# Where the down lows, the first block's weight sums, the token loads and the normalising of a conv-FFN stand on their engines

## The reference, cut to what matters

```python
def conv_ffn(h, conv_hist, w_up, w_dw, b_dw, w_down):
    up = h @ w_up                                   # 1024 -> 2 * 2816
    ext = jnp.concatenate([conv_hist.astype(up.dtype), up], axis=1)
    c = ext[:, 0:T] * w_dw[0] + ext[:, 1:T + 1] * w_dw[1] + ext[:, 2:T + 2] * w_dw[2] + b_dw
    a, b = jnp.split(c, 2, axis=-1)
    return (jax.nn.silu(a) * b) @ w_down, ...       # 2816 -> 1024
...
    x2 = layer_norm(ALPHA * x1 + ffn + ple, ln2_g, ln2_b)
```

## Time and profile before

| what | us |
|---|---|
| median of 3 runs (lowest, highest) | 3042.74 (3041.82, 3044.16) |
| the profiled execution | 3045.18 |
| its span, first to last instruction | 3043.4 |
| busy in the span: PE, DVE, ACT, POOL | 2853.6, 2110.9, 1451.0, 1066.3 |

### The profile page before, as it was taken

One profiled execution on the slowest core, in us unless ns is written; L12 is line 12 of the kernel. 1 busy time (PEld: TensorE's weight loads), 2 busy tenths in 40 slices (PEclk: granted clock), 3 DMA queues, 4 the chain that ended last, 5 costly groups with the idle time before them and its releaser, 6 DMA issues. The chain is left out here.

```text
span 3043.4 us, 47351 instructions
## 1 busy us (share of the span) xinstructions
PE 2853.6 (94%) x14597; PEld 2481.4 (82%) x14597; DVE 2110.9 (69%) x3081; ACT 1451.0 (48%) x2947; POOL 1066.3 (35%) x816
## 2 busy tenths in 40 slices
PE   8998999999999899999899999988999997999996
PEld 6877787777777688887798988878999996888885
DVE  5635776777776444445687877797777778788776
ACT  4342555877787222222453444443544544455553
POOL 5341544766676433334433333210111111111113
PEclk9997998999999999999999999989999998999998
DMA  4226452222113333334633324344323334533331
GB/s 136 87 69 145 139 167 56 43 62 47 43 43 129 129 104 103 103 103 147 206 108 103 118 91 133 116 142 161 100 93 117 100 94 137 183 121 119 107 119 58
DMA packets 234859, 333.26 MB, mean 110 GB/s; under 512 B 66897, under 2 KB 109617, under 8 KB 233361
## 3 DMA queue, kind: packets, MB, share of 16 engines
q1 hardware_dynamic: 234736, 331.76, 35.5%
HBM read 246.05 MB, written 85.63 MB: 109 GB/s over the span
## 5 line engine op out<-in xcount | busy, mean ns | idle before, releaser
L3053 DVE TENSOR_TENSOR mx_w_lo<-ff_w_raw,mx_w_hi 128x512 fp32r<-128x512 f32 x390 | 312.3, 827 | 23.8 <-ACT mx_w_hi L2867 23.7
L2767 POOL TENSOR_TENSOR mx_odd<-ff_d_raw,mx_odd 128x512 fp32r<-128x512 f32 x66 | 91.5, 1386 | 596.1 <-ACT mx_odd L2876 595.4
L2867 ACT ACTIVATE mx_w_hi<-ff_w_raw 128x512 fp32r<-128x512 f32 x390 | 232.7, 622 | 33.9 <-POOL ff_w_raw L2755 33.9
L3110 DVE TENSOR_TENSOR ho_raw<-ho_raw,ff_d 128x512 f32<-128x512 f32 x264 | 168.3, 681 | 114.4 <-PE ff_d L86 110.0
L1567 POOL TENSOR_TENSOR at_p_lo<-at_p,at_p_hi 128x512 fp32r<-128x512 f32 (+2 forms) x160 | 187.6, 1173 | 164.1 <-ACT at_p_hi L1604 162.5
L2876 ACT ACTIVATE mx_odd<-ff_d_raw 128x512 fp32r<-128x512 f32 x66 | 41.5, 629 | 395.1 <-PE ff_d L86 389.7
L1597 ACT ACTIVATE at_p<-at_s 128x512 f32<-128x512 f32 (+1 forms) x320 | 169.9, 531 | 111.6 <-PE at_s L1793 56.4
L1709 DVE TENSOR_TENSOR at_p_lo<-at_p,at_p_hi 128x512 fp32r<-128x512 f32 (+1 forms) x160 | 187.3, 1171 | 45.2 <-ACT at_p_hi L1604 44.3
L84 PE MATMUL ff_d<-mx_odd,ff_h_hi 128*128 128x512 f32 x364 | 146.7, 403 | 40.5 <-DVE ho_raw L3110 30.2
L1604 ACT ACTIVATE at_p_hi<-at_p 128x512 fp32r<-128x512 f32 (+1 forms) x320 | 179.0, 560 | 0.0
L3086 DVE SCALAR_TENSOR_TENSOR ff_cv_a<-ff_up_a,ff_taps,ff_cv_a 128x768 f32<-128x768 f32 (+1 forms) x132 | 123.3, 934 | 55.5 <-ACT ff_cv_a L2933 28.2
(11 more groups left out here) (558 smaller groups left out, 9860.2 us busy)
## 6 DMA issues: line engine op xcount, KB each, us to landing
ff_w_raw<-in_w_ffn_p SPq DMA_DIRECT2D x216, 256.0 KB, 3.5
ff_w_raw<-scratch_sums SPq DMA_DIRECT2D x176, 256.0 KB, 3.5
ff_d_raw<-in_w_ffn_p SPq DMA_DIRECT2D x132, 256.0 KB, 2.8
scratch_sums<-ff_w_raw SPq DMA_DIRECT2D x84, 256.0 KB, 3.5
ho_raw<-in_x SPq DMA_DIRECT2D x17, 512.0 KB, 4.1
mx_m_raw<-scratch_mix_t SPq DMA_DIRECT2D x17, 512.0 KB, 5.2
scratch_x_t<-mx_work SPq DMA_DIRECT2D x17, 512.0 KB, 2.6
scratch_y<-mx_work SPq DMA_DIRECT2D x17, 512.0 KB, 2.9
```

Of the source, the lines that this page charges most:

```text
L2767: pool.tensor_tensor(lo, d_raw[:, :], f32(hi), ALU.subtract).then_inc(dlo, 1)
L2867: act.activation(w[j][0], raw, ACT.Copy).then_inc(whi, 1)
L3053: dve.tensor_tensor(w[j][1], raw, f32(w[j][0]), ALU.subtract).then_inc(wlo_dve, 1)
L3110: dve.tensor_tensor(y[t][:, H[i]], y[t][:, H[i]], ps_d[2 * (t % 2) + i][:, :], ALU.add)\
```

## The change

Five things are moved; no arithmetic is added or taken out.

1. Down lows go from GpSimd to VectorE, 4 per pair in all blocks. Pieces 1 and 3 come after the A22 and A11 lows, piece 2 ahead of `join` 3, piece 0 after `join` 3. In the last pair of block 2 piece 0 comes before piece 1 in the odd slice.
2. Block 0's sums from f = 3 on go from GpSimd to VectorE: four between `join` 1 and `join` 2 of the even slice, and S3, S1, S2 of the one after between `add` 2 and `add` 3, with S4 in the odd slice. `add` 0 to 2 of block 0 come between the S2, S1 and S3 lows.
3. At a block change the loads of B11 and B21 come ahead of the load of down piece 2; ScalarE copies product S3 before it takes B11's hi and takes piece 3's hi earlier; in slices 1 and 2 of blocks 1 and 2 it copies S2 earlier (`early`).
4. Normalising moves from slices 0 and 1 to slices 1 and 2, and `add` waits for each y tile by itself (`y_in[t]`).
5. ScalarE's S4 hi moves from `finish_up` to behind `carry_in`.

```diff
@@ sync
-                sp.dma_start(y[t], g["y0"][r:r + P, :]).then_inc(y_in, 16)
+                sp.dma_start(y[t], g["y0"][r:r + P, :]).then_inc(y_in[t], 16)
...
             def odd_loads(b, f, p, at_next, at_d, turning=False):
-                turn = isinstance(f, int) and f == FT - 1
+                turn = isinstance(f, int) and f == FT - 1 and b < 2
+                if turn:
+                    load_x(b + 1, B11)
+                    load_x(b + 1, B21)
                 load_down(b, p, at_d, 2)
                 for j in range(PRODUCTS):
-                    if turn and b < 2:
+                    if turn and j > 1:
                         load_x(b + 1, j)
...
@@ gpsimd
-            even(0, 0, 0)
-            odd(0, 1, 0)
-            for b in range(3):
...
-            down_lows(2, LAST, (3,))
+            combine(0, 2, 1, 0)
+            for b in range(2):
+                root(b, range(BLOCKS[b]))
...
@@ scalar
                 copy(b, f, par, 3)
-                if nb < 3:
-                    weights(nb, nf, (S4,))
                 begin(b, f, p, i, 1)
...
                 carry_in(b, f, p, i, 0)
                 if before is not None:
+                    weights(b, f, (S4,))
                     weights(b, f, (A22,), p, i)
                     activate(*before[:4])
+                if begins and b > 0:
+                    down_highs(before[0], before[2], (3,))
...
+                early = b > 0 and isinstance(f, int) and f in (1, 2)
+                if early:
+                    copy(b, f, i, 1)
                 if before is not None:
                     product_hi(*before[:4])
...
+                copy(b, f, i, 2)
                 if x_next:
                     tokens(b + 1, (B11,))
-                copy(b, f, i, 2)
...
@@ vector
             def add(b, p, t):
+                if isinstance(p, int) and p == 0:
+                    dve.wait_ge(y_in[t], 16 * (b + 1))
...
+            def combine(b, f, pf, par, ops=range(4)):
...
+            def down_lows(b, p, parts):
+                for m in parts:
+                    dve.wait_ge(dhi, down_n(b, p, m))
+                    hi, lo = down_piece(b, p, m)
+                    dve.tensor_tensor(lo, d_raw[:, :], f32(hi), ALU.subtract).then_inc(dlo, 1)
...
                     weights(b, f, (S4,), par)
+                    if begins:
+                        down_lows(b - 1, LAST, (3,))
                     hidden_low(*before)
                     join(b, f, par, 0)
                     weights(b, f, (A22,), par)
+                    if b == 0 and par == 1 and not (isinstance(f, int) and f in (1, FT - 1)):
+                        combine(0, f + 1, p + 1, 0, (3,))
...
+                    if at_end(b, p) and par == 1:
+                        down_lows(b, p, (0,))
-                    weights(nb, nf, (A11, A12) if more else ())
+                    weights(nb, nf, (A11,) if more else ())
+                    if par == 1:
+                        down_lows(b, p, (1,))
+                    elif not begins:
+                        down_lows(before[0], before[2], (3,))
+                    weights(nb, nf, (A12,) if more else ())
...
                 join(b, f, par, 1)
+                if b == 0 and par == 0 and not begins:
+                    combine(0, f + 1, p, 1)
+                join(b, f, par, 2)
...
+                if b == 0 and par == 0 and adds is not None:
+                    add(*adds, 0)
+                weights(nb, nf, (S2,) if more else ())
...
+                if par == 1:
+                    down_lows(b, p, (2,))
+                elif b == 0 and adds is not None:
+                    add(*adds, 1)
+                    weights(nb, nf, (S1,))
+                    add(*adds, 2)
+                    weights(nb, nf, (S3,))
+                    if not (isinstance(f, int) and f == FT - 2):
+                        combine(0, f + 2, p + 1, 0, (0, 1, 2))
+                    for t in range(3, BLOCKS[b]):
+                        add(*adds, t)
...
                 join(b, f, par, 3)
                 if more and par == 1:
                     weights(nb, nf, (S1, S3))
+                if par == 0 and not at_end(b, p):
+                    down_lows(b, p, (0,))
...
-                       norm=((), (), (0, 1)) if b else none)
-                period(b, 1, 1, (b, 0, 0, 0), norm=((2,), (3,), (4, 5)) if b else none)
+                period(b, 0, 0, 0, (b - 1, FT - 1, LAST, 1) if b else None)
+                period(b, 1, 0, 1, (b, 0, 0, 0), norm=((0,), (1, 2), (3,)) if b else none)
+                period(b, 2, 1, 0, (b, 1, 0, 1), adds=(b, 0), norm=((4,), (5,), ()) if b else none)
...
             convolve(2, FT - 1, LAST, 1, 0)
+            down_lows(2, LAST, (3,))
             add(2, LAST - 1, 0)
```

More of the change, by code:

```diff
@@ L2426, in ffn @@
         d_in = sem("d_in")
-        y_in, st_y, st_c = sem("y_in"), [sem(f"st_y{t}") for t in range(BLOCKS[0])], sem("st_c")
+        y_in, st_y = ([sem(f"{n}{t}") for t in range(BLOCKS[0])] for n in ("y_in", "st_y"))
+        st_c = sem("st_c")
         combined, whi = sem("combined"), sem("whi")
@@ L2648, in even_loads @@
             def even_loads(b, f, p, at_next, at_d, turning=False):
+                next_loads(b, f, p, 0, at_next, () if b == 0 else (A11, A22))
+                load_down(b, p, at_d, 0)
                 if turning:
                     load_y(b, 3)
[L2652 to L2659, removed]
+                    store_y(b - 1, 4)
                 if b == 0:
@@ L2664, in even_loads @@
                 next_loads(b, f, p, 0, at_next, (A12,))
-                next_loads(b, f, p, 0, at_next, (S2, S1, S3))
+                if turning and BLOCKS[b] > 4:
+                    load_y(b, 4)
+                next_loads(b, f, p, 0, at_next, (S2,))
+                if turning:
+                    for t in range(5, BLOCKS[b - 1]):
+                        store_y(b - 1, t)
+                    for t in range(5, BLOCKS[b]):
+                        load_y(b, t)
+                next_loads(b, f, p, 0, at_next, (S1, S3))
                 load_down(b, p, at_d, 1)
@@ L2761, in combine @@
                     pool.tensor_tensor(s4, a12, s2, ALU.subtract).then_inc(combined, 1)
[L2763 to L2767, removed]
             def tokens(b, roles):
@@ L2994, in period @@
                     tokens(b, (T3,))
-                copy(b, f, i, 1)
+                if not early:
+                    copy(b, f, i, 1)
                 if i == 1:
                     down_highs(b, p, (1,))
-                elif before is not None:
+                elif before is not None and not begins:
                     down_highs(before[0], before[2], (3,))
@@ L3043, in _ @@
             dve.sem_inc(hlo, 1)
+            dve.sem_inc(dlo, 4)
             dve.sem_inc(mul, 1)
@@ L3138, in normalise, with stored, period @@
                        .then_inc(shifted, 1)
-            def period(b, f, par, before, adds=None, x_next=False, after_last=False, norm=((), (), ())):
+            def combine(b, f, pf, par, ops=range(4)):
+                pb, pf_ = following(b, f, -1)
+                def stored(j):
+                    if not (isinstance(f, int) and f == 1):
+                        dve.wait_ge(sums_out[j], 16 * (f - 1))
+                a11, a12, s1, a22 = w_raw[:, A11, :], w_raw[:, A12, :], w_raw[:, S1, :], raw22(par)
+                s2, s3, s4 = w_raw[:, S2, :], w_raw[:, S3, :], w_raw[:, S4, :]
+                if 0 in ops:
+                    dve.wait_ge(combined, sum_n(pb, pf_, 3))
+                    dve.wait_ge(raw_in[A11], 16 * (b * FT + f + 1))
+                    dve.wait_ge(raw_in[S1], 16 * (b * FT + f + 1))
+                    dve.wait_ge(*low_done(pb, pf_, S3))
+                    stored(S3)
+                    dve.tensor_tensor(s3, a11, s1, ALU.subtract).then_inc(combined, 1)
+                    dve.wait_ge(combined, sum_n(b, f, 0))
+                    dve.wait_ge(raw_in22[par], 16 * (b * PAIRS_F + pf + 1))
+                    dve.tensor_tensor(s1, s1, a22, ALU.add).then_inc(combined, 1)
+                    dve.wait_ge(combined, sum_n(b, f, 1))
+                    dve.wait_ge(*low_done(pb, pf_, S2))
+                    stored(S2)
+                    dve.tensor_tensor(s2, s1, a11, ALU.subtract).then_inc(combined, 1)
+                if 3 in ops:
+                    dve.wait_ge(combined, sum_n(b, f, 2))
+                    dve.wait_ge(raw_in[A12], 16 * (b * FT + f + 1))
+                    dve.wait_ge(*low_done(pb, pf_, S4))
+                    stored(S4)
+                    dve.tensor_tensor(s4, a12, s2, ALU.subtract).then_inc(combined, 1)
+            def down_lows(b, p, parts):
[3 more added lines that the diff above has]
+                    dve.tensor_tensor(lo, d_raw[:, :], f32(hi), ALU.subtract).then_inc(dlo, 1)
+            def period(b, f, p, par, before, adds=None, x_next=False, norm=((), (), ())):
                 nb, nf = following(b, f, 1)
@@ L3165, in period @@
                     normalise(b - 1, norm[0])
```

(2 more changed lines are left out.)

74 lines of the change are left out of this document (19 added, 55 removed).

## The result

The kernel after takes 3058.18 us (3057.24 to 3061.34), the kernel before, beside it on the same chip, 3044.1 us (3041.82 to 3048.52). The ratio is 1.0048, 95% interval 1.0033 to 1.0063: slower by half a per cent, 14 us, where 3033 and a gain were forecast and the range ended at 3052. The profiled execution of after has a span of 3059.6 us, that of before 3043.4, so 16.2 us are to be found.

The account below looks back on a forecast made before the run. TensorE was taken to bound only block 1, with waits elsewhere. Block 0 -11, changes -16, block 1 +1.5, block 2 +13, tail +4.5, opening -1.5 sum to -9.5 on 3042.74: 3033 us, range 2998 to 3052.

Parts of the forecast that it names:

- The mechanism that decided: Slower rival, chance 0.2: the chain through the down lows decides, 2.0 us later in blocks 1 and 2; 3051 us.
- the down-low loop: In a pair: low 1, load, hi, low 2, `join` 3, `begin`, convolution, gate, hidden low, low 3, down product.
- Block 1: Piece 3's low comes 1.6 to 1.8 us later against 1.4 of cover: 0.2 per pair, +1.5 us (0 to +5).
- a cover of 1.4: In block 1 before the change, down lows end 1.4 us ahead of the down product.
- S4's hi: On ScalarE: has cover, since VectorE uses it only after the gate; uncovered it would cost 0.6 us at most.
- Block 2: Same two delays of the down lows without cover: down product 1.5 us later per pair, +13 us (+5 to +20).
- Block 0: Sums on VectorE: stall before tile 2 nearly gone, new one before tile 5; gain 1.1 per pair, -11 us (0 to -29).
- The terms that were listed: Block 0's losses per pair: 0.2 us old stall before tile 2, 1.2 new stall, 0.3 later down product, 0.3 restart.
- The changes: Both block changes: copy wait gone, most of piece 3's low wait gone, y loads spread; -8 us each, -16 (-4 to -27).
- opening: Opening of block 0: piece 1's load no longer waits behind GpSimd's sums; -1.5 us (-4 to +1).
- tail: Last pair: piece 0 on VectorE 4 us later, piece 3 before `add` 0 adds 0.6; +4.5 us (+1 to +6).
- The faster rival: Chance 0.25: TensorE-bound again, S1's load in time and down lows hidden; block 0 gives 28, changes 8 each; 2999 us.

Follow-up runs that it names:

- the lows first: Kernel after with VectorE's lows of pieces 1 and 3 moved up directly behind `join` 0: 3016.27 us, ratio 0.99 to the kernel before.
- The two last runs: Kernel after with S4's hi in its old place and f+2 sums behind `add` 3; down lows early on VectorE: 2997.73 us, or back on GpSimd: 3000.22 us.
- Three reorderings: Kernel after with lows 1 and 3 behind `join` 0, S4's hi in its old place, block 0's f+2 sums behind `add` 3: 2997.73 us, ratio 0.9836.
- the best version: Kernel after with lows 1 and 3 behind `join` 0, S4's hi in its old place, block 0's f+2 sums behind `add` 3: 2997.73 us.

## Why the prediction was wrong

The sign was wrong, and the time lay 6 us above the range. The mechanism that decided was among the rivals, at a chance of 0.2 and 7 us too cheap. The step that failed is the price of the down-low loop: too small in blocks 1 and 2, and next to nothing in block 0.

**Block 1: the delay was mis-sized.** The prediction had low 3 come 1.6 to 1.8 us later, against a cover of 1.4. The cover was right. The delay is 2.7 (44.1 to 46.8 us behind D). Against the pair of before that ends at 2252.83, in which low 3 ended 43.9 behind D, it is 2.9 and adds up. The two steps that were priced came out as priced: the places of low 1 and low 3 cost 0.86 and 0.87. The rest was left out: S4's hi delays SiLU and so both gates, 0.24 and 0.30; `join` 3, which the text put behind low 2 and gave no price, 0.26; the load of piece 2 reached ScalarE 2.6 us after its issue, where in that pair it took 2.3 (in the pairs beside it 2.5 to 2.6), 0.36. Together 1.7 + 1.2. Past the cover each 0.1 us costs 0.1 in every pair: 1.3, and the restarts.

**S4's hi: the cover was not there.** The prediction asked when VectorE uses that hi, and found it after the gate. It did not ask what stands behind the hi on ScalarE, which is SiLU, and the gate waits for SiLU. The run with it in its old place gives 0.3 to 0.6 per pair.

**Block 2: the same error without a cover.** 1.5 us a pair were forecast, 2.64 measured, +20 instead of +13. Moved back one at a time, low 1 is worth 1.2 us, where the prediction put 0.8, low 3 0.8 to 1.1, where it put 0.9, and S4's hi 0.3, where it put nothing. The +20 is the upper end of the step's bounds, where the sum took the middle.

**Block 0: the loop was forgotten.** The stall before tile 2 went, the one before tile 5 came at 1.07 to 1.30 (1.2 was forecast), and with the lows first the pair is 47.58, near the forecast 47 to 47.5. But D was made later by 0.3 only, as if the loop that was priced for blocks 1 and 2 did not run in block 0. It costs 49.17 - 47.58 = 1.6 there, and the gain of 11 became a loss of 4. (The terms that were listed, 0.2, 1.2, 0.3 and 0.3, add up to a loss of 2.0 of 2.9 and a gain of 9, not 11.) That step's bounds, 0 to -29, left no room for a loss, so the range had none for it either.

**The changes, opening and tail came out near the forecast.** -17.7 for the two changes, where -16 was forecast. The fit of the sum is in part luck: it is -12.0 and -5.7, not -8 each, and the loads, copies and normalising that the forecast went by give only -11.3 of it, the down lows on VectorE most of the rest. The wait for the copy is gone, the wait for T2's token is 4.09, 3 to 4 forecast, and TensorE's wait for the `join` 3 that normalising holds up is 5.46, in change 1:

```profile
1983.51 0.66 PE L84 MATMUL ff_u<-mx_odd,mx_w_hi 128*128 128x384 f32 x1 [4.09 <-DVE mx_odd L3033]
...
2040.22 0.69 PE L84 MATMUL ff_uz<-ho_hi,mx_w_hi 128*128 128x384 f32 x1 [5.46 <-DVE ff_up_a L3047]
```

The opening gave 4.2 where 1.5 was forecast (bounds to -4), the tail lost 2.6 where 4.5 was (bounds from 1).

**For the down lows the exchange of engines alone is worth nothing that can be told.** The Trainium skill, Perfetto Trace Analysis, section Optimizing Scalar/DVE Operations, has it that moving work between VectorE and GpSimd might not help because they share a port. The two last runs agree: in a good order 2997.73 and 3000.22, intervals overlapping. The prediction read the same rule as an exchange at no loss and got 3014 from it; that failed on the order of the instructions, of which the rule says nothing.

**The faster rival lay in the same code.** 2999 us was given for TensorE-bound loops in blocks 0 and 1. Three reorderings, with the work on the engines that the change chose, give 2997.73. What that version leaves is in the changes, where TensorE still idles some 20 and 24 us, and in block 2's wait for copy 0, 1.3 to 1.7 us in a pair; no run was made on either.

## What to carry to other kernels

Where work is passed round several engines within one loop, follow one chain from a release back to itself, add every instruction and wait on it, and hold the sum against the pace of the bounding engine: the difference is the slack, and past it each instruction put ahead of a link costs its whole length in every round, in every stage that runs the loop. Ask of a moved instruction first what stands behind it on its new engine, then who uses it. The wait that a profile names is the last one only: here it stayed at 0.6 us while the pair grew from 46.9 to 47.5.

## What the runs showed of the hardware that was not expected

A stall of TensorE costs more than the idle time that the profile shows. The prediction put 0.3 us on it in block 0 and nothing in blocks 1 and 2. In the pair of block 1 above TensorE waits 0.31 and 0.61, 0.92 in all, and the pair is 46.97 - 45.51 = 1.46 longer: 0.54 more for two restarts, at a granted clock of 1.00. The starts of the products show most of it: 2.08 us from product to product without a wait, 2.55 with the wait of 0.31 between (0.16 over), 2.99 with that of 0.61 (0.30 over, of which 0.12 are the first matmuls behind the wait before). The ends of matmuls are modelled in the profile, so how the loss divides into waiting and restarting is not shown; its sum is.

VectorE at 86% busy over 414 us (block 0 of the best version) still let TensorE run with 1 us idle, while at 74% (block 1 of after) it cost 7: the busy share told nothing of which order would hold TensorE up.
